# A two-block transformer kernel on one core: every tile of its scratch arena lies 32 bytes further in each partition

## The chip, the cores and the metric

The kernel runs on one NeuronCore of a Trainium2 chip. Its time is the device time of that core in microseconds (us). Two runs of the kernel before took 2086.70 and 2087.92 us, median 2087.31 us. The matmul engine (PE) has a granted clock with two levels, 2.4 GHz (shown as 1.00) and 1.2 GHz (0.50).

## The reference

Two blocks, each of two layers, over 256 tokens of width 1024; everything is float32.

```python
def reference(x, c, ctx, ...):
    x = first_block(x, c, ctx, c_ctx, w_ada, ..., w_mlp1, w_mlp2)
    return second_block(x, hyb_w_in_2, ..., ln2_g_2, ln2_b_2)

# first_block, for each of 2 layers (the 256 context tokens go along in the first, and give keys and values in the second):
#   modulation vectors   silu(c) @ w_ada[i] + b_ada[i]
#   px = modulate(rmsnorm(x)) @ w_in[i]       # conv input, q, k, v, gates
#   differential attention, conformer conv (31 taps, depthwise), gated merge, @ w_out
#   x = x + gx2 * square(relu(h @ w1)) @ w2
# second_block: layer 0 a hybrid mixer (sliding window attention + gated delta rule),
#   layer 1 a recurrent mixer (4-tap conv, gated linear scan); each followed by
#   layer_norm(alpha * x + mix) and layer_norm(alpha * x + square(relu(x @ w1)) @ w2)
```

## The kernel before

All weights stream from HBM as 273 chunks of 1 MiB through a ring of four slots, `raw_weights`. Each float32 chunk is split in two: ScalarE (ACT, L1363) rounds it to `weights_hi` in the type float32r, and VectorE (DVE, L1964) writes the rest, `weights_lo`, over the raw slot. The modulation chunks alone are used raw. Activations are split in the same way (`h_hi` and `h_lo`, and likewise o, z, ff, g, xc). A product is then three float32r matmuls into one PSUM bank: hi by hi (L652), hi by lo (L653), lo by hi (L654). The other matmuls (attention scores and values, transposes, the delta rule, the warm-up matmuls `keep_warm` at L705) are plain float32.

A matmul has a stationary operand, loaded into the array, and a moving operand, streamed through it. There are three shapes of product:

- `gemm_T` and `first_gemm`: a 128x128 piece of the weights is stationary, the activations move, 512 or 256 columns.
- `gemm_M`: a 128x128 piece of the activations is stationary, 256 columns of weights move.
- `acc_chunks` (L1017, L1018, L1021; the second block's down projections and output projections): a piece of the activations is stationary, 512 columns of weights move.

The order on each engine is written out by hand, with semaphores between the engines and hardware loops over the MLP steps. SyncE issues the chunks' transfers, each when its slot is free. No planner or cost table decides anything.

Where the tiles lie matters here. The long-lived tiles are allocated one after the other, and the allocator rounds each start up to 32 bytes. After them comes the arena, 112 KiB in each partition, in which the tiles of the stages overlay each other at whole or half KiB; its base is rounded up to 64 bytes:

```python
ARENA = 112 * 1024
arena_at = -(-nc.sbuf_base // 64) * 64

def place(name, kib, shape, dt=F32):
    size = 4 * int(np.prod(shape[1:]))
    assert kib * 1024 + size <= ARENA, (name, kib, size)
    return nc.alloc_sbuf_tensor_at(name, shape, dt, offset=int(arena_at + kib * 1024))
```

The byte addresses in a partition, worked out from these sizes:

| tile | address | past a multiple of 64 |
|---|---|---|
| raw_weights, weights_lo | 16,512 | 0 |
| weights_hi | 49,280 | 0 |
| xT (the residual tokens) | 82,048 | 0 |
| cols, rows | 98,432; 100,896 | 0; 32 |
| consts (identity, ones, tables) | 105,568 | 32 |
| small, ssq, qprod, osq_row, root | 111,136 to 112,544 | 32 |
| arena base | 114,624 | 0 |
| arena end | 229,312 | 0 |

In the arena are, among others, h_hi, h_lo, qT, kT, val, z, zc, qs, exA, exT, o_hi, o_lo, ff, ffsq, ff_hi, ff_lo, g_hi, g_lo, masks, xr, xc, outrow. Slices of these that matmuls use start at multiples of 256 bytes from the tile's start, so all of them start at a multiple of 64. VectorE's convolutions don't: z has rows of 286 elements (1,144 bytes) and its 31 taps (L2198) start 4 bytes apart; cx and xr have rows of 259 elements (1,036 bytes), four taps each (L2518, L2728), and are written 12 bytes into each row (L1710 by ACT).

Of the kernel before, what the change touches and what calls it, by code (L numbers as in the profile page):

```python
# [239 lines left out]
def build_program(nc, a):  # L240
    with ExitStack() as ctx:
# [23 lines left out]


        ARENA = 112 * 1024
        arena_at = -(-nc.sbuf_base // 64) * 64

        def place(name, kib, shape, dt=F32):  # L270
            size = 4 * int(np.prod(shape[1:]))
# [2734 lines left out]
```

## Time and profile before

| | |
|---|---|
| median of the runs | 2087.31 us |
| the profiled execution (its span, first to last instruction) | 2089.1 us |
| PE busy, share of the span | 2024.6 us, 97% |
| PE's weight loads busy | 1789.9 us, 86% |
| DVE busy | 1363.7 us, 65% |
| ACT busy | 1019.1 us, 49% |
| POOL busy | 162.3 us, 8% |
| mean granted PE clock | 0.991 |
| DMA | 294.56 MB, mean 141 GB/s |

The first line is the metric. The profiled execution is one run of the same program; no time beside its span is recorded for it, and 2089.1 is 1.8 us above the median. PE's spans overlap each other, since matmuls are pipelined, so the pace of a stream of matmuls is read from the distance between their starts, not from the duration of one.

### The profile page before, as it was taken

The page shows a single profiled execution, that of the slowest core. Times are in us where ns is not written, and L with a number is a line of the kernel's source. Part 1 is how long each engine was busy: PE and PEld are TensorE (multiplying, and loading weights), DVE is VectorE, ACT ScalarE, POOL GpSimd, SP SyncE. Part 2 cuts the span into 40 slices and gives each one's busy share as a digit, 9 for nine tenths or more (in the row PEclk, how much of TensorE's full clock was granted, in tenths as well). Part 3 has the DMA queues.
Part 4 walks back from the last instruction along what each step waited for, and adds up shares of the span by engine and source line. Part 5 has one row for each costly group of instructions (what it writes and reads, how often), then busy time and mean ns, then how long its engine had stood idle before and what let it go on. Part 6 is the DMA issues. An engine that isn't in the chain of part 4 may idle for free.

```text
span 2089.1 us, 36236 instructions
## 1 busy us (share of the span) xinstructions
PE 2024.6 (97%) x13946; PEld 1789.9 (86%) x13946; DVE 1363.7 (65%) x2114; ACT 1019.1 (49%) x2014; POOL 162.3 (8%) x174
## 2 busy tenths in 40 slices
PE   6999999999999999999999999999999999999998
PEld 5899657888788888879967999999998989888897
DVE  5699688344565564577977667776766555886455
ACT  5475575324422322358457454445824444675443
POOL 0000000000000001000000002223120111000110
PEclk9999999999999999999999999999999999999999
DMA  7322374222222222233255545554302555443553
GB/s 287 122 82 102 122 283 161 81 101 101 81 83 98 100 100 83 98 108 135 83 203 217 179 147 181 185 192 176 115 21 82 181 181 188 184 164 137 191 183 121
DMA packets 40896, 294.56 MB, mean 141 GB/s; under 512 B 4544, under 2 KB 4544, under 8 KB 5456
## 3 DMA queue, kind: packets, MB, share of 16 engines
q1 hardware_dynamic: 40464, 290.73, 38.4%
q0 software_dynamic: 320, 2.26, 0.3%
q8 instruction: 79, 1.29, 0.3%
q14 instruction: 33, 0.27, 0.0%
HBM read 291.93 MB, written 1.05 MB: 140 GB/s over the span
## 4 chain that ended last, share of the span: by engine, by line
PE 88%; DVE 5%; ACT 4%; issue 1%; DMA 1%; SPq 0%; DVEq 0%; ACTq 0%
PE psum L652 21%; PE psum L654 21%; PE psum L653 20%; PE psum L1017 3%; PE psum L1021 3%; PE psum L1018 3%; PE psum L890 2%; PE psum L1224 2%; DVE weights_lo L1964 2%; PE psum L793 2%; PE psum L912 1%; PE psum L692 1%; PE psum L693 1%; PE psum L694 1%; ACT weights_hi L1363 1%
## 5 line engine op out<-in xcount | busy, mean ns | idle before, releaser
L1964 DVE TENSOR_TENSOR weights_lo<-raw_weights,weights_hi 128x2048 fp32r<-128x2048 f32 x225 | 512.6, 2291 | 163.1 <-ACT weights_hi L1363 162.7
L1363 ACT ACTIVATE weights_hi<-raw_weights 128x2048 fp32r<-128x2048 f32 x225 | 429.0, 1910 | 152.6 <-DMA raw_weights<-in_weights 133.1
L2043 DVE SCALAR_TENSOR_TENSOR xT<-psum,mods,xT 128x256 f32<-128x256 f32 x408 | 181.0, 479 | 199.9 <-PE psum L654 196.5
L652 PE MATMUL psum<-h_hi,weights_hi 128*128 128x512 f32 (+1 forms) x832 | 279.9, 336 | 0.1
L654 PE MATMUL psum<-h_lo,weights_hi 128*128 128x512 f32 (+1 forms) x832 | 279.8, 336 | 0.0
L653 PE MATMUL psum<-h_hi,weights_lo 128*128 128x512 f32 (+1 forms) x832 | 278.1, 334 | 0.0
L2840 POOL TENSOR_TENSOR ffsq<-ff 128x256 f32<-128x256 f32 (+1 forms) x128 | 118.2, 925 | 1592.1 <-ACT ff L1450 1107.6
L652 PE MATMUL psum<-weights_hi,h_hi 128*128 128x256 f32 x704 | 197.5, 280 | 0.0
L653 PE MATMUL psum<-weights_lo,h_hi 128*128 128x256 f32 x704 | 195.5, 278 | 0.0
L654 PE MATMUL psum<-weights_hi,h_lo 128*128 128x256 f32 x704 | 195.5, 278 | 0.0
L652 PE MATMUL psum<-g_hi,weights_hi 128*128 128x256 f32 x688 | 193.7, 282 | 0.0
L654 PE MATMUL psum<-g_lo,weights_hi 128*128 128x256 f32 x688 | 192.7, 280 | 0.0
L653 PE MATMUL psum<-g_hi,weights_lo 128*128 128x256 f32 x688 | 192.5, 280 | 0.0
L652 PE MATMUL psum<-ff_hi,weights_hi 128*128 128x512 f32 (+1 forms) x512 | 172.9, 338 | 0.3 <-DVE xT L2043 0.3
L654 PE MATMUL psum<-ff_lo,weights_hi 128*128 128x512 f32 (+1 forms) x512 | 172.1, 336 | 0.0
L653 PEld LDWEIGHTS psum<-h_hi,weights_lo 128*128 128x128 f32 x832 | 156.3, 188 | 17.6
L654 PEld LDWEIGHTS psum<-h_lo,weights_hi 128*128 128x128 f32 x832 | 156.2, 188 | 17.3
L653 PE MATMUL psum<-ff_hi,weights_lo 128*128 128x512 f32 (+1 forms) x512 | 170.8, 334 | 0.0
L652 PEld LDWEIGHTS psum<-h_hi,weights_hi 128*128 128x128 f32 x832 | 156.0, 188 | 16.8 <-ACT ff L1450 0.8
L1450 ACT ACTIVATE ff<-psum 128x512 f32<-128x512 f32 (+1 forms) x64 | 31.4, 491 | 273.9 <-PE psum L654 271.6
L652 PEld LDWEIGHTS psum<-weights_hi,h_hi 128*128 128x128 f32 x704 | 132.6, 188 | 0.3 <-issue 0.2
L653 PEld LDWEIGHTS psum<-weights_lo,h_hi 128*128 128x128 f32 x704 | 132.5, 188 | 0.3 <-issue 0.2
(423 smaller groups left out, 4277.6 us busy)
## 6 DMA issues: line engine op xcount, KB each, us to landing
raw_weights<-in_weights SPq DMA_DIRECT2D x273, 1024.0 KB, 4.8
staged_x<-in_x_rows SPq DMA_DIRECT2D x1, 2048.0 KB, 10.0
masks<-in_masks POOLq DMA_DIRECT2D x1, 1152.0 KB, 6.8
ln_rows<-in_ln_rows POOLq DMA_DIRECT2D x1, 1024.0 KB, 6.8
out<-outrow SPq DMA_DIRECT2D x4, 256.0 KB, 2.1
rows<-in_rows SPq DMA_DIRECT2D x1, 584.0 KB, 9.7
consts<-in_consts SPq DMA_DIRECT2D x1, 388.0 KB, 3.8
cols<-in_cols SPq DMA_DIRECT2D x1, 306.0 KB, 2.8
```

What stands on the lines that cost most here:

```text
L652: mm(out, *pair(wh, vh), start=i == 0, stop=False)
L653: low = mm(out, *pair(wl, vh), start=False, stop=False)
L654: last = mm(out, *pair(wh, vl), start=False, stop=i == len(terms) - 1)
L793: last = mm(out[j:j + QUAD, :], cond[:, k, :], ws[c][:, k, :], start=k < 2, stop=k >= KT - 2, tile_position=(0, j))
L890: last = mm(b, qT[64 * c:64 * c + 64, h, q * P:q * P + P], kT[64 * c:64 * c + 64, h, k0 * P:k1 * P], start=True, stop=True)
L1017: mm(out, h, wh[:, k, n], start=False, stop=False)
L1018: low = mm(out, h, wl[:, k, n], start=False, stop=False)
L1021: last = mm(out, lo, wh[:, k, n], start=False, stop=final and k0 == k0s[-1] and k == 1)
L1363: f(w_hi[:, s, :], raw[:, s, :], ACT.Copy).then_inc(hi_done, 1)
L1964: tt_(w_lo[:, s, :], raw[:, s, :], w_hi[:, s, :].bitcast(F32), ALU.subtract).then_inc(lo_done, 1)
L2043: last = stt(xT[:, m, c], b[:, c], mods[:, l, which + m, v:v + 1], xT[:, m, c], ALU.mult, ALU.add)
L2840: tt_(ffsq[:, par, m, 0:T], x, x, ALU.mult).then_inc(ff_squared, 1)
```

## The change

The base of the arena is moved by 32 bytes. Sizes, overlays, instructions and their order stay as they are on every engine (7140 instructions in PE's program text, 1131 in DVE's, 871 in ACT's, 107 in POOL's, 25 in SP's, before and after); only the addresses of the arena's tiles differ. The base is 114,656 instead of 114,624, and the end 229,344. The tiles ahead of the arena (the weights' ring, xT, the constants) stay where they are.

```diff
@@ -265,7 +265,7 @@
         ARENA = 112 * 1024
-        arena_at = -(-nc.sbuf_base // 64) * 64
+        arena_at = -(-nc.sbuf_base // 64) * 64 + 32
 
         def place(name, kib, shape, dt=F32):
             size = 4 * int(np.prod(shape[1:]))
```

## Rows read from the trace of the kernel before

**Rows 1.** The page, part 1: busy us, share of the span, instructions.
```profile
PE 2024.6 (97%) x13946; PEld 1789.9 (86%) x13946; DVE 1363.7 (65%) x2114; ACT 1019.1 (49%) x2014; POOL 162.3 (8%) x174
```

**Rows 2.** The page, part 4: the chain that ended last, share by engine.
```profile
PE 88%; DVE 5%; ACT 4%; issue 1%; DMA 1%; SPq 0%; DVEq 0%; ACTq 0%
```

**Rows 3.** PE by form; out<-moving,stationary, rows*columns loaded, moving shape, count | busy us, mean ns.
```profile
L652 PE MATMUL psum<-weights_hi,h_hi 128*128 128x256 f32 x704 | 197.5, 280 | 0.0
...
L652 PE MATMUL psum<-g_hi,weights_hi 128*128 128x256 f32 x688 | 193.7, 282 | 0.0
...
L652 PE MATMUL psum<-h_hi,weights_hi 128*128 128x512 f32 x416 | 163.4, 393 | 0.0
...
L652 PE MATMUL psum<-h_hi,weights_hi 128*128 128x256 f32 x416 | 116.5, 280 | 0.1
...
L652 PE MATMUL psum<-ff_hi,weights_hi 128*128 128x512 f32 x256 | 101.4, 396 | 0.0
L1017 PE MATMUL psum<-weights_hi,ff_hi 128*128 128x512 f32 x256 | 100.9, 394 | 0.0
...
L652 PE MATMUL psum<-ff_hi,weights_hi 128*128 128x256 f32 x256 | 71.5, 279 | 0.3 <-DVE xT L2043 0.3
```

**Rows 4.** Timeline of PE, activations moving, 512 columns; start us first.
```profile
799.52 0.39 PE L653 MATMUL psum<-ff_hi,weights_lo 128*128 128x512 f32 x1
...
803.18 0.39 PE L654 MATMUL psum<-h_lo,weights_hi 128*128 128x512 f32 x1
```

**Rows 5.** Timeline of PE, activations moving, 256 columns, first layer's second half.
```profile
1169.62 0.28 PE L652 MATMUL psum<-o_hi,weights_hi 128*128 128x256 f32 x1
...
1171.98 0.28 PE L654 MATMUL psum<-o_lo,weights_hi 128*128 128x256 f32 x1
```

**Rows 6.** The same form (256 columns of activations) in the hybrid mixer.
```profile
1454.77 0.28 PE L653 MATMUL psum<-g_hi,weights_lo 128*128 128x256 f32 x1
...
1456.92 0.28 PE L654 MATMUL psum<-g_lo,weights_hi 128*128 128x256 f32 x1
```

**Rows 7.** Timeline of PE in an `acc_chunks`: weights moving, 512 columns.
```profile
1637.82 0.40 PE L1017 MATMUL psum<-weights_hi,ff_hi 128*128 128x512 f32 x1
...
1640.86 0.39 PE L1018 MATMUL psum<-weights_lo,ff_hi 128*128 128x512 f32 x1
```

**Rows 8.** Timeline of PE, plain float32, both operands in the arena.
```profile
1532.30 1.06 PE L1224 MATMUL psum<-tIT,ut 128*128 128x128 f32 x8
1533.19 1.06 PE L1224 MATMUL psum<-ut,tIT 128*128 128x128 f32 x8
```

**Rows 9.** Timeline of PE, plain float32, warm-up matmuls: both operands in consts.
```profile
1608.79 1.28 PE L705 MATMUL psum<-consts 128*128 128x128 f32 x10
```

**Rows 10.** Instructions of single lines: count, ns min/median/max, first and last start.
```profile
L2198 DVE SCALAR_TENSOR_TENSOR zc<-z,cols,zc x240: 473/608/951, 68.2 to 1049.1; 128x512 f32<-128x512 f32 x60, 128x256 f32<-128x256 f32 x60
L2728 DVE SCALAR_TENSOR_TENSOR xc<-xr,cols,xc x24: 466/472/480, 1812.0 to 1829.7; 128x256 f32<-128x256 f32 x24
L1710 ACT ACTIVATE cx<-psum x12: 361/385/390, 1449.3 to 1499.3; 128x256 f32<-128x256 f32 x12
L1511 ACT ACTIVATE kT<-psum x16: 365/384/388, 158.1 to 1021.5; 128x256 f32<-128x256 f32 x16
```

**Rows 11.** The page, part 6: DMA issues, KB each, median us to landing.
```profile
staged_x<-in_x_rows SPq DMA_DIRECT2D x1, 2048.0 KB, 10.0
...
out<-outrow SPq DMA_DIRECT2D x4, 256.0 KB, 2.1
...
consts<-in_consts SPq DMA_DIRECT2D x1, 388.0 KB, 3.8
cols<-in_cols SPq DMA_DIRECT2D x1, 306.0 KB, 2.8
```

**Rows 12.** Timeline of PE while its clock was granted at half speed.
```profile
1440.68 0.41 PE L652 MATMUL psum<-weights_hi,g_hi 128*128 128x256 f32 x1
...
1442.81 0.41 PE L653 MATMUL psum<-weights_lo,g_hi 128*128 128x256 f32 x1
```

## The prediction

> **What bounds the kernel.** I began with the busy shares [rows 1]: PE is busy for 97% of the span, and no other engine for more than 65%. The chain of waits says the same from the other side [rows 2]: 88% of the path that ended last is PE's own work, 5% DVE's, 4% ACT's, 1% transfers. So an address can cost time in two ways only: it changes the pace of matmuls, or it lengthens a DVE, ACT or DMA step of the remaining 10%. Third came the groups of PE by form [rows 3]. In those rows the reader should see which operand moves. The three lines of `product` repeat each other's counts, so activations move with 512 columns in 3 x (416 + 256 + 96) = 2,304 matmuls, where 96 is the o tiles' smaller group, and in 2,592 once the groups of `first_gemm` and z are added; with 256 columns in 3 x (688 + 416 + 256 + 96) = 4,368, and 4,896 with the smaller groups. Weights move with 256 columns in 3 x 704, 2,352 in all, and with 512 columns in 3 x 256, 959 in all. That is 10,799 float32r matmuls, and each has exactly one operand in the arena: moving in 7,488 of them, stationary in 3,311. Last, the timeline gives the pace of each form by its starts.
>
> **The paces.** Activations moving, 512 columns: 16 intervals in 803.18 - 799.52 = 3.66 us, 228.8 ns each [rows 4]. The same, 256 columns: 20 intervals in 2.36 us, 118.0 ns [rows 5]. But the same form also runs at 19 intervals in 2.15 us, 113.2 ns [rows 6]. Weights moving, 512 columns: 13 intervals in 3.04 us, 233.8 ns [rows 7]. Two things follow. A column costs (228.8 - 118.0) / 256 = 0.433 ns, which leaves 118.0 - 256 x 0.433 = 7.2 ns of fixed cost in a matmul. And an identical form has two paces 4.8 ns apart, so something beside the columns decides between them; the operands of [rows 5] and [rows 6] both lie at multiples of 64 bytes, so that something is not visible in these starts.
>
> **The change, part by part.** No instruction is added, removed or moved, so each term is a change in the duration of something that is there.
>
> *Plain float32 matmuls.* Before the change, consts already lies 32 bytes past a multiple of 64, so the trace holds the case that the change creates. With both operands in the arena, eight matmuls start 1533.19 - 1532.30 = 0.89 us before the next eight: 111 ns each [rows 8]. Warm-up matmuls with both operands in consts: 10 in 1.28 us; with the last one's 275 ns ((1.06 - 0.275) / 7 = 112 ns is the same reckoning on the arena's eight) that is (1.28 - 0.275) / 9 = 112 ns [rows 9]. A start at 32 costs neither the stationary nor the moving operand anything here. Term: 0, bounds plus or minus 1 ns on some 1,600 matmuls, 1.6 us.
>
> *Float32r matmuls.* No float32r operand lies at 32 before, so this is bounded by neighbours. The nearest row is again the plain float32 one, which reads 128 columns in 112 ns; the float32r one reads 256 columns in 113 to 118 ns, so it asks about twice as much of the memory per ns, if a plain column is read once. That is the gap through which a cost could come. I take the nearest row's value, 0. Upper end: one more unit of reading in each matmul, the line rival below; lower end: the fixed cost, below too.
>
> The Trainium skill ("SBUF — State Buffer", Specifications) says that SBUF's lines are 16 bytes, that two hits per line are needed, and that each crossing to a new line pays. A shift of 32 bytes leaves every element at the same place in its line, so by that rule the float32r term is 0 as well; no row here shows the size of a line for a float32r stream.
>
> *DVE and ACT.* The convolutions already read at every multiple of 4 bytes within 64. L2728's 24 instructions take 466 to 480 ns over their different starts, and L2198's two forms show no second level beyond a lone slow one (its minimum 473 is that of the 256-column form) [rows 10]. ACT writes cx at twelve different starts in 361 to 390 ns, and kT, whose starts are all multiples of 64, in 365 to 388. Term: 0. As a bound, 14 of 480 ns is 3%; on the 9% of the span that DVE and ACT have in the chain (188 us) that is plus or minus 5.6 us. The large splits of the chunks (L1363, L1964) lie outside the arena and don't change, whatever DVE does on arena tiles. POOL's tiles have no such row, but POOL is idle for 92% of the span [rows 1] and is no part of the chain; a few per cent on its squares stay hidden behind PE's up projection.
>
> *DMA.* The 273 chunks land outside the arena. In it land staged_x, on the path for 10.0 us, the masks and ln_rows, early and unwaited, and out leaves from it, its last part on the path for 2.1 us. consts (at 32) landed at 388 / 3.8 = 102 KB/us, cols (at 0) at 306 / 2.8 = 109 [rows 11], so 7% at most of 12.1 us: 0 to 0.9 us. I take 0.
>
> **Sum.** 2089.1 + 0 = 2089.1 us for the profiled execution, which stands 1.8 us (0.1%) above the median of the runs. I forecast 2087 us.
>
> **The rivals.** 2% of this kernel is 42 us, and is about what a measurement of it can tell from no change; the first rival stays below it.
>
> *The two paces trade places* (22%). What puts a form at 113.2 or 118.0 ns could be how its two streams of reads, the stationary and the moving, fall against each other, and that changes when one of them moves by 32 bytes and the other doesn't. For it: the two paces exist in one form [rows 5, 6]. Against it: they exist with nothing moved. If all 256-column matmuls with moving activations fell to the faster pace, 4,896 x 4.8 ns = 24 us, and the 959 weight streams went from 233.8 to 228.8, another 5 us: 2089 - 28 = 2061. If instead 2,352 weight streams went up by 4.8 ns (11 us) and 2,592 of 512 columns by 5.0 ns (13 us): 2113. Both ends are extremes.
>
> *One reading unit more in each matmul* (13%), the case on the slower side. Suppose PE fetches a float32r stream in pieces of 64 bytes, 16 columns. A start in the middle of a piece makes every stream touch one piece more, 16 x 0.433 = 6.9 ns. Place: PE, in each matmul whose activations move, 7,488 x 6.9 ns = 52 us, 2141 us; if weight loads pay too, 10,799 x 6.9 = 75 us, 2164. It decides once the fetch has no slack left, which plain float32 at half the columns per ns can't tell. Against it: all of [rows 8, 9] show not even 1 ns.
>
> *The stream runs at a fraction of its pace* (6%): every piece is fetched twice and the array starves. The far end is the pace that the row at half clock shows, 10 intervals in 2.13 us, 213 ns for 256 columns [rows 12]. For 4,896 that is +95 ns, 465 us, and for 2,592 of 512 columns twice as much, 492 us: 3046. A tenth of it gives 2185.
>
> *Faster by over 2%* (4%): the fixed 7.2 ns vanish, because the two reads no longer meet. 10,799 x 7.2 = 78 us: 2011.
>
> That the change doesn't do what it says I give nothing: the arena ends at 229,344, and all addresses in it follow from the one base.
>
> **How the numbers follow.** No change within some 8 us: 55%. With the trade of paces within 2%: 77%. Slower by over 2%: 13 + 6 = 19%. Faster by over 2%: 4%. The range goes from 2061, the low end of the trade of paces, to 2141, the line rival without the weight loads, which takes in about half of its 13%; outside are the other half, the 6% and the 4%, some 17%.
>
> **What would show it.** Right: 118 and 229 ns between starts in the same stages, 112 for plain float32 with arena operands, PE busy 2025 us, staged_x landing in 10 us. A trade of paces shows as 113 where 118 was, or the reverse, stage by stage. The line rival shows as 125 and 236 where activations move, and no change, or the same 7 ns, where weights move; plain float32 stays at 112. A fraction of the pace shows in matmul durations above 280 and 393 ns. The forecast fails if float32r reading has a unit coarser than 32 bytes that plain float32 doesn't feel.

## The result, and the profile after

The changed kernel takes 2118.86 us (median of 2 runs, 2117.6 to 2120.11) where the kernel before took 2087.31: 1.0144 times as long, with a 95% interval of 1.0119 to 1.0169. That is 31.6 us more. By the 2% bound it counts as no change; by its own interval it is slower. The profiled execution has a span of 2118.3 us against 2089.1, so 29.2 us more, and it is this difference that the traces have to explain.

Part 1 of the page gives busy us, share of the span and instructions:

```profile
PE 2058.0 (97%) x13946; PEld 1810.1 (85%) x13946; DVE 1360.7 (64%) x2114; ACT 1019.6 (48%) x2014; POOL 162.8 (8%) x174
```

Against [rows 1] the counts are the same on every engine, DVE lies 3.0 us lower, ACT and POOL 0.5 higher. PE alone is busy for 33.4 us more, and its weight loads for 20.2 us more. The chain of waits, by engine, and the landing of the first transfer:

```profile
PE 87%; DVE 7%; ACT 4%; issue 1%; DMA 1%; DVEq 0%; SPq 0%; ACTq 0%
```

```profile
staged_x<-in_x_rows SPq DMA_DIRECT2D x1, 2048.0 KB, 10.4
```

The chain is still PE's [rows 2]. staged_x lands 0.4 us later than in [rows 11], no more than a detail of 29 us. So the matmuls themselves became longer. The groups by form (out<-moving,stationary, count, busy us, mean ns of one) say where. These answer to [rows 3]:

```profile
L652 PE MATMUL psum<-weights_hi,h_hi 128*128 128x256 f32 x704 | 199.2, 283 | 0.0
...
L652 PE MATMUL psum<-g_hi,weights_hi 128*128 128x256 f32 x688 | 195.3, 284 | 0.0
...
L652 PE MATMUL psum<-h_hi,weights_hi 128*128 128x512 f32 x416 | 163.6, 393 | 0.0
L652 PE MATMUL psum<-h_hi,weights_hi 128*128 128x256 f32 x416 | 117.9, 283 | 0.1
...
L1017 PE MATMUL psum<-weights_hi,ff_hi 128*128 128x512 f32 x256 | 101.4, 396 | 0.0
```

The 256-column groups have a mean 2 or 3 ns higher, but the 512-column group of h has the 393 ns of [rows 3] (its two sister groups in L653 and L654 rose from 389 and 393 to 394 and 399). A reader who stopped at this row would think the wide matmuls untouched. They aren't: the mean duration holds a matmul's whole latency, and matmuls overlap, so a stream's cost is the distance between starts. The timeline of PE, activations moving, 512 columns (start us, us, line, operands):

```profile
812.08 0.39 PE L653 MATMUL psum<-ff_hi,weights_lo 128*128 128x512 f32 x1
...
816.28 0.39 PE L653 MATMUL psum<-ff_hi,weights_lo 128*128 128x512 f32 x1
```

18 intervals in 4.20 us are 233.3 ns each, where [rows 4] gave 228.8. The same with 256 columns:

```profile
1190.62 0.28 PE L652 MATMUL psum<-o_hi,weights_hi 128*128 128x256 f32 x1
...
1192.78 0.28 PE L652 MATMUL psum<-o_hi,weights_hi 128*128 128x256 f32 x1
```

18 intervals in 2.16 us, 120.0 ns, against 118.0 in [rows 5]. With the roles exchanged, weights moving with 256 columns, first the kernel before (a form not shown so far) and then the changed one:

```profile
149.70 0.28 PE L652 MATMUL psum<-weights_hi,h_hi 128*128 128x256 f32 x1
...
151.96 0.28 PE L654 MATMUL psum<-weights_hi,h_lo 128*128 128x256 f32 x1
```

```profile
149.95 0.28 PE L652 MATMUL psum<-weights_hi,h_hi 128*128 128x256 f32 x1
...
152.41 0.28 PE L652 MATMUL psum<-weights_hi,h_hi 128*128 128x256 f32 x1
```

20 intervals in 2.26 us are 113.0 ns, and 21 in 2.46 us are 117.1. Plain float32 stays where it was: the warm-up matmuls of [rows 9] read

```profile
1635.26 1.28 PE L705 MATMUL psum<-consts 128*128 128x128 f32 x10
```

the same 1.28 us for ten. Adding up the distances from one start to the next over all recorded float32r matmuls gives the account of the 29.2 us:

| form | count | before, us | after, us | typical ns between starts |
|---|---|---|---|---|
| activations move, 512 columns | 2,592 | 598.1 | 610.1 (+12.0) | 229.0 to 233.4 |
| activations move, 256 columns | 4,896 | 592.5 | 600.2 (+7.7) | 117.8 (some 113.3) to 120.0 |
| weights move, 256 columns | 2,352 | 274.4 | 282.5 (+8.1) | 113.3 (some 117.8) to 117.4 or 118.8 |
| weights move, 512 columns | 959 | 226.2 | 226.7 (+0.5) | 233.3 to 233.9 |
| all | 10,799 | 1691.3 | 1719.6 (+28.3) | |

28.3 of the 29.2 us lie there. The half-clock stretches are no part of it: of 38.3 us at half the granted clock before, 16.5 lay in float32r distances, and of 43.9 after, 14.4. The 0.9 us that are left are the balance of small terms outside these matmuls, of the clock among others, and no run takes them apart.

### The profile page after: what moved, and what is told of

The parts are those of the page before. It is cut to its first block, busy times and chain, and to the rows that moved or that the text cites. A ratio compares the mean times of both kernels' runs of the same rounds, so it can differ in the third digit from the quotient of the medians.

```text
span 2118.3 us, 36236 instructions
## 1 busy us (share of the span) xinstructions
PE 2058.0 (97%) x13946; PEld 1810.1 (85%) x13946; DVE 1360.7 (64%) x2114; ACT 1019.6 (48%) x2014; POOL 162.8 (8%) x174
## 3 DMA queue, kind: packets, MB, share of 16 engines
q0 software_dynamic: 320, 2.26, 0.3%
## 4 chain that ended last, share of the span: by engine, by line
PE 87%; DVE 7%; ACT 4%; issue 1%; DMA 1%; DVEq 0%; SPq 0%; ACTq 0%
PE psum L654 20%; PE psum L652 20%; PE psum L653 20%; PE psum L1017 3%; PE psum L1018 3%; PE psum L1021 3%; DVE weights_lo L1964 2%; PE psum L890 2%; PE psum L1224 2%; PE psum L793 2%; PE psum L912 1%; ACT weights_hi L1363 1%; PE psum L692 1%; PE psum L694 1%; PE psum L693 1%
## 5 line engine op out<-in xcount | busy, mean ns | idle before, releaser
L654 PE MATMUL psum<-h_lo,weights_hi 128*128 128x512 f32 (+1 forms) x832 | 283.6, 341 | 0.0
L653 PE MATMUL psum<-h_hi,weights_lo 128*128 128x512 f32 (+1 forms) x832 | 280.5, 337 | 0.0
L654 PE MATMUL psum<-weights_hi,h_lo 128*128 128x256 f32 x704 | 197.2, 280 | 0.0
L653 PE MATMUL psum<-weights_lo,h_hi 128*128 128x256 f32 x704 | 197.2, 280 | 0.0
L654 PE MATMUL psum<-g_lo,weights_hi 128*128 128x256 f32 x688 | 194.8, 283 | 0.0
L653 PE MATMUL psum<-g_hi,weights_lo 128*128 128x256 f32 x688 | 194.2, 282 | 0.0
L654 PE MATMUL psum<-ff_lo,weights_hi 128*128 128x512 f32 (+1 forms) x512 | 174.6, 341 | 0.0
L653 PEld LDWEIGHTS psum<-h_hi,weights_lo 128*128 128x128 f32 x832 | 157.3, 189 | 20.1
L653 PE MATMUL psum<-ff_hi,weights_lo 128*128 128x512 f32 (+1 forms) x512 | 172.6, 337 | 0.0
L654 PEld LDWEIGHTS psum<-h_lo,weights_hi 128*128 128x128 f32 x832 | 155.9, 187 | 18.1
L653 PEld LDWEIGHTS psum<-weights_lo,h_hi 128*128 128x128 f32 x704 | 132.6, 188 | 0.3 <-issue 0.2
```

Source lines behind the costliest of these rows:

```text
L653: low = mm(out, *pair(wl, vh), start=False, stop=False)
L654: last = mm(out, *pair(wh, vl), start=False, stop=i == len(terms) - 1)
```

## The experiments

Three theories went into the first round. **A**: a float32r operand's own start decides, in either role, so a start at 32 past a multiple of 64 is slow in itself. **B**: what decides is how the moving and the stationary start lie to each other. **C**: the pace comes from outside PE (other engines or transfers that use the same memory), and the addresses matter only through them. Below, d is the moving start minus the stationary start in bytes, modulo 256. Weights come from a ring at 16,512 (128 modulo 256), the arena lies at 114,624 (192), and its float32r tiles at multiples of 1,024 from there. So before the change d is 64 where activations move and 192 where weights move; after it d is 96 and 160.

### e1_bench

PE by itself, in streams built like the kernel's. T(m, s, n): activations move from start m, weights stationary from s, n columns; M: weights move; PL: plain float32. Each case is one line, 48 matmuls, all bases being equal modulo 256.

```
def T(mov, stat, n, reps=2):  # as gemm_T: weights stationary
    for m in range(reps):
        c = slice(m % 2 * P, m % 2 * P + P)
        terms = [(W(stat, 0, 256 * k, c), W(stat, 1, 256 * k, c), H(mov, 0, k, slice(0, n)), H(mov, 1, k, slice(0, n)))
                 for k in range(KT)]
        for x in product(terms, True):
            yield (psum[:, m % 2, 0:n], *x)
...
for o, w, v, first, end in T(64, 0, 512): last = mm(o, w, v, start=first, stop=end)
for o, w, v, first, end in T(96, 0, 512): last = mm(o, w, v, start=first, stop=end)
for o, w, v, first, end in T(0, 0, 512): last = mm(o, w, v, start=first, stop=end)
for o, w, v, first, end in T(32, 0, 512): last = mm(o, w, v, start=first, stop=end)
...
for o, w, v, first, end in T(64, 32, 512): last = mm(o, w, v, start=first, stop=end)
for o, w, v, first, end in T(96, 32, 512): last = mm(o, w, v, start=first, stop=end)
```

> PE alone: no other engine works while it runs, and the output is no result of the blocks (all of their computation is left out). Each line is one stream of float32r matmuls with the slices' addresses of the real kernel: T is gemm_T (weights stationary, activations moving), M is gemm_M; the first number is how many bytes the moving operand starts past a multiple of 128, the second the same of the stationary one. Theory A (own start): a float32r stream pays when its own start is not at a multiple of 64, in either role. Then T(96, 0, 512) is 233 ns between starts and T(64, 0, 512) 229, T(64, 32, 512) is slower than 229 as well, T(96, 32, 512) is the slowest, T(0, 0) equals T(64, 0), and T(32, 0), T(80, 0), T(68, 0) are like T(96, 0). Theory B (relative): what counts is how the moving and the stationary stream lie against each other. Then T(96, 32) equals T(64, 0), and T(64, 32) equals T(96, 0). Theory C (other engines): the loss needs traffic of the other engines; then all T of one width are alike here. Plain float32 (PL) is 112 ns at every start by all three.

Measured, timeline of PE. L86 to L89 are T(64,0), T(96,0), T(0,0) and T(32,0) with 512 columns, L92 and L93 are T(64,32) and T(96,32), L94 is T(64,0) with 256; L113 to L115 are plain float32 at (64,0), (96,0) and (96,32), two records a matmul:

```profile
43.46 11.15 PE L86 MATMUL psum<-hid,wgt 128*128 128x512 f32 x48
54.45 11.37 PE L87 MATMUL psum<-hid,wgt 128*128 128x512 f32 x48
65.66 11.07 PE L88 MATMUL psum<-hid,wgt 128*128 128x512 f32 x48
76.57 11.37 PE L89 MATMUL psum<-hid,wgt 128*128 128x512 f32 x48
...
110.21 11.35 PE L92 MATMUL psum<-hid,wgt 128*128 128x512 f32 x48
121.40 11.15 PE L93 MATMUL psum<-hid,wgt 128*128 128x512 f32 x48
132.39 5.81 PE L94 MATMUL psum<-hid,wgt 128*128 128x256 f32 x48
...
262.15 10.88 PE L113 MATMUL psum<-plain 128*128 128x128 f32 x96
272.87 10.88 PE L114 MATMUL psum<-plain 128*128 128x128 f32 x96
283.59 10.88 PE L115 MATMUL psum<-plain 128*128 128x128 f32 x96
```

A group's duration holds 47 intervals and one whole matmul, so L86 is (11.15 - 0.39) / 47 = 228.9 ns and L87 (11.37 - 0.39) / 47 = 233.6. Those are the kernel's two numbers with DVE, ACT and POOL idle and 0 to 2 GB/s of transfers, so C falls. Moving both operands by 32, L93, brings 228.9 back, where A wanted the slowest of all, so A falls; T(32,0) is as slow as T(96,0). T(0,0), with the roundest starts of all, has yet another pace, about 227. With 256 columns: 117.8 for T(64,0), 119.9 for T(96,0), and where weights move 113.3 for M(0,64) and 120.0 for M(0,96). The last is not quite the kernel's number after the change (117.4 or 118.8) at the same distance; the scan below shows 117.1 for it. Plain float32 doesn't feel it: 10.72 us from each start to the next, 111.7 ns a record.

### e2_both32

The pair of operands keeps its distance, and everything lies 32 bytes further: the change, with the ring moved along.

```diff
+        sb("pad", [P, 8])
-        ring_at = -(-nc.sbuf_base // 64) * 64
+        ring_at = -(-nc.sbuf_base // 32) * 32
...
-        arena_at = -(-nc.sbuf_base // 64) * 64
+        arena_at = -(-nc.sbuf_base // 64) * 64 + 32
```

> The change with the weights' ring, xT and the constants also 32 bytes further, so that both operands of all 10,799 float32r matmuls start at 32 past a multiple of 64. Theory A (own start): both streams pay, slower than the change's 2119 us, 2125 to 2150. Theory B (relative placement): the two lie against each other as before the change, 2087 us, with the paces 229 and 118 ns.

Measured: 2090.17 us, 1.0008 (0.9997 to 1.0019) times the kernel before, which had 2088.57 in this and the next two experiments. Page and timeline:

```profile
PE 2024.4 (97%) x13946; PEld 1789.5 (86%) x13946; DVE 1363.1 (65%) x2114; ACT 1018.8 (49%) x2014; POOL 161.9 (8%) x174
```

```profile
799.77 0.39 PE L654 MATMUL psum<-h_hi,weights_lo 128*128 128x512 f32 x1
...
803.89 0.39 PE L654 MATMUL psum<-h_hi,weights_lo 128*128 128x512 f32 x1
```

PE's 2024.6 us of [rows 1] are back within 0.2, and 18 intervals in 4.12 us are 228.9 ns again. The whole arena lies where the change put it, and costs nothing there. A had expected 2125 to 2150 us. This is the run that decides against it in the kernel itself: DVE, ACT and the transfers have the changed addresses here too, and the time is that of before.

### e3_ring32

The opposite: the arena stays, the ring moves by 32.

```diff
+        sb("pad", [P, 8])
-        ring_at = -(-nc.sbuf_base // 64) * 64
+        ring_at = -(-nc.sbuf_base // 32) * 32
```

> The arena where it was before the change, at a multiple of 64, and the weights' ring (with xT and the constants) 32 bytes further: the roles of the change turned round. Theory A (own start): weights that move pay (959 x 4.4 + 2,352 x 2.2 = 9 us) and stationary weights pay in up to 7,488 matmuls at up to 4 ns (30 us), 2096 to 2126 us. Theory B (relative): as the change, 2119 us, and with the change's paces in each form: 233 ns where 512 columns of activations move.

Measured: 2108.23 us, 1.0095 (1.0079 to 1.011).

```profile
PE 2045.5 (97%) x13946; PEld 1797.0 (85%) x13946; DVE 1361.7 (65%) x2114; ACT 1019.5 (48%) x2014; POOL 162.5 (8%) x174
```

```profile
812.00 0.39 PE L654 MATMUL psum<-ff_hi,weights_lo 128*128 128x512 f32 x1
...
816.20 0.39 PE L654 MATMUL psum<-ff_hi,weights_lo 128*128 128x512 f32 x1
```

No arena address differs from the kernel before, and yet PE is busy for 20.9 us longer. Of these, 14.5 us are float32r distances, and about 6.4 are half of the 12.9 us more that this execution spent at half the granted clock (51.2 against 38.3). The run alone doesn't exclude A, whose range for it (2096 to 2126 us) holds the measured time; e1_bench and e2_both32 do. The 512-column streams run at 4.20 / 18 = 233.3 ns as in the changed kernel. But B had expected the change's full cost, 2119 us, and missed. By the medians it came out at two thirds, and the float32r distances grow by 14.5 us and not 28.3, because 256-column streams of activations ran at 116.7 ns, faster than before, where the change has 120.0. So the distance decides, but not by whether it is an odd multiple of 32: 32 and 224 are other cases than 96 and 160. That asked for a scan, e5_scan.

### e4_ff32

One pair of tiles is moved, ff_hi and ff_lo, all else as before.

```diff
-        ffH = place("ff_hi", 48, [P, 2, 2, T2], F32R)
-        ffL = place("ff_lo", 56, [P, 2, 2, T2], F32R)
+        ffH = place("ff_hi", 48 + 1 / 32, [P, 2, 2, T2], F32R)
+        ffL = place("ff_lo", 56 + 1 / 32, [P, 2, 2, T2], F32R)
```

> The kernel before with ff_hi and ff_lo alone 32 bytes further. They move in 768 matmuls of 512 columns and 768 of 256, and are stationary in 768 of 512 columns. With the differences between the two traces (+4.4 ns, +2.2, +0.6) that is 3.4 + 1.7 + 0.5 = 5.6 us, 2093 us, by theories A and B alike, and every other tile's matmuls keep 229 and 118 ns. If the loss came from the phase of the whole program, or from another engine's tiles, 2087 us.

Measured: 2095.99 us, 1.0041 (1.0028 to 1.0054); by the medians 7.4 us, where 5.6 were expected. In the trace the streams with ff have the paces of the changed kernel (233.3 ns for 768 of 512 columns, 120.0 for 768 of 256, 234.1 where weights move), and h, g, o, z and xc those of before (229.0 and 117.8 for h). All float32r distances together grow by 5.8 us; from the paces, 768 x 4.4 + 768 x 2.2 + 767 x 0.8 ns = 5.7. The cost belongs to the pair of tiles that a matmul reads, and not to a state of the core as a whole.

### e5_scan

PE alone again, 24 matmuls each, every multiple of 32 up to 480, finer steps, and S: as T with 32 or 64 stationary columns.

```
cases=["T(64, 0, 512, 4)"]
for f,n in (('T',512),('T',256)):
    cases+=[f"{f}({m}, 0, {n}, 1)" for m in scan]
for n in (256,512):
    cases+=[f"M(0, {s}, {n}, 1)" for s in scan]
...
for n in (512,256):
    for cols in (32,64):
        cases+=[f"S({m}, 0, {n}, {cols})" for m in (0,32,64,96,68)]
```

> PE alone again (all of the blocks' computation is left out). The relative start is scanned: moving minus stationary from 0 to 480 bytes in steps of 32 for T (512 and 256 columns), stationary minus moving for M, then finer steps, then T with only 32 or 64 stationary columns (S). If the pace depends on the difference with a period of 128 bytes, T(128), T(256), T(384) equal T(0) = 226.6 ns, and T(192), T(320), T(448) equal T(64) = 228.8; with a longer period they differ. If two reads that meet are the cause, a shorter weight read meets the stream less: with 32 stationary columns every start comes within 2 ns of 216 ns for 512 columns; if the moving stream alone were the cause, S(96, 0, 512, 32) keeps 233 ns against 229 of S(64, 0, 512, 32).

Measured, timeline of PE: L94 to L97 are d = 0, 32, 64, 96, L98 is 128, L102 to L106 are 256, 288, 320, 352 and 384, all with 512 columns:

```profile
43.61 5.63 PE L94 MATMUL psum<-hid,wgt 128*128 128x512 f32 x24
49.08 5.77 PE L95 MATMUL psum<-hid,wgt 128*128 128x512 f32 x24
54.68 5.67 PE L96 MATMUL psum<-hid,wgt 128*128 128x512 f32 x24
60.18 5.77 PE L97 MATMUL psum<-hid,wgt 128*128 128x512 f32 x24
65.80 5.76 PE L98 MATMUL psum<-hid,wgt 128*128 128x512 f32 x24
...
88.21 5.63 PE L102 MATMUL psum<-hid,wgt 128*128 128x512 f32 x24
93.67 5.77 PE L103 MATMUL psum<-hid,wgt 128*128 128x512 f32 x24
99.28 5.67 PE L104 MATMUL psum<-hid,wgt 128*128 128x512 f32 x24
104.78 5.77 PE L105 MATMUL psum<-hid,wgt 128*128 128x512 f32 x24
110.39 5.76 PE L106 MATMUL psum<-hid,wgt 128*128 128x512 f32 x24
```

5.63, 5.77, 5.67, 5.77, 5.76 us, and the same five from 256 on, while 128 (5.76) is not 0 (5.63): the pattern repeats after 256 bytes and not after 128. So do the 256-column streams (d = 192 and 448: the same 113.3 ns). In ns between starts, over the second half of each stream, since the first matmuls are still settling (over all 23 intervals d = 0 has 227.8):

| d, bytes | 0 | 32 | 64 | 96 | 128 | 160 | 192 | 224 |
|---|---|---|---|---|---|---|---|---|
| 512 columns | 226.7 | 233.3 | 228.9 | 233.3 | 233.3 | 234.3 | 233.3 | 233.3 |
| 256 columns | 120.0 | 117.7 | 117.8 | 120.1 | 118.7 | 117.3 | 113.3 or 117.8 | 118.3 |

With the roles exchanged the 512-column row is the same function of d: M(0,192), d = 64, gives 228.9, M(0,64), d = 192, 233.3, M(0,96), d = 160, 234.2. With 256 columns too M(0,160), d = 96, has 120.0 and M(0,96) 117.1, but there a distance doesn't always give one pace: d = 160 ran at 120.0 in the first experiment, and d = 192 at 113.3 in T and 117.8 in M. Off the multiples of 32 it goes further: 236.7 ns at d = 4, 240.0 at 68, which in the first experiment ran at 236.7. The table turns e3_ring32's miss round. For d = 32 it has 233.3 and 117.7, for 224 it has 118.3 and 233.3, and that kernel showed 233.3, 116.7, 118.3 and 233.3. The streams with fewer stationary columns answered nothing. With 32 of them the 512-column streams ran at 231.5, 233.5, 231.7 and 233.3 ns (d = 0, 32, 64, 96), neither all alike nor as with 128, and nowhere near the 216 ns that were expected. With 512 columns the differences become smaller when less is loaded; with 256 columns they don't (32 stationary columns: 113.3 ns at d = 0 and 64, 117 at 32 and 96). That part is inconclusive.

### e6_d0

By the table the roundest choice, d = 0 in all streams, is best for 512 columns and worst for 256. The arena goes to 114,560; for that the four columns of lam move into cols.

```diff
-        cols = sb("cols", [P, COLS_N])
+        cols = sb("cols", [P, COLS_N + 4])
-        lam = sb("lam", [P, 4])
+        lam = cols[:, COLS_N:COLS_N + 4]
-            sp.dma_start(cols[:, :], a["cols"]).then_inc(loaded, 16)
+            sp.dma_start(cols[:, 0:COLS_N], a["cols"]).then_inc(loaded, 16)
```

> The arena 64 bytes lower, at 114,560, a multiple of 128 (lam is kept in four spare columns of cols to make room), so that activations and weights start at the same place in 256 bytes. If the pace is a function of moving minus stationary start modulo 256 and nothing else, as the scan with PE alone gave it (E5), the difference is 0 in every float32r matmul: 226.7 ns where 512 columns of activations move (-2.2 x 2,592 = -5.7 us), 120.0 where 256 columns of activations move (+2.2 x 4,896 = +10.8), 120.0 where 256 of weights move (+5.3 x 2,352 = +12.4), 226.7 where 512 of weights move (-6.6 x 959 = -6.3): +11 us, ratio 1.0054, slower although the base is at a rounder address. If a rounder start is what helps (theory A with a unit of 128), 2087 or faster.

Measured: 2098.83 us, 1.0059 (1.0038 to 1.008), where the table had given 1.0054; the kernel before had 2089.23 in this and the next two.

```profile
800.03 0.39 PE L652 MATMUL psum<-h_hi,weights_hi 128*128 128x512 f32 x1
...
803.88 0.39 PE L654 MATMUL psum<-h_lo,weights_hi 128*128 128x512 f32 x1
```

17 intervals in 3.85 us, 226.5 ns: the wide streams gain 2, as in L88 of the first experiment, and all 256-column ones go to 119.9, which costs more. The profiled execution is shorter than the median says (span 2091.1) for a reason of its own: it spent 24.9 us at half the granted clock where the profile of before spent 38.3. Its float32r distances stand only 7.4 us above before's. Of the time at half clock 6.5 and 16.5 us lay in them, so (16.5 - 6.5) / 2 = 5.0 us more would be there at equal clock, 12.4 in all where the table had 11.2. This is the first run that turns the paces of the bench into a forecast of the kernel, and it held; of the three that follow, two missed.

### e7_ff192

Now the table is used to gain. ff is read at 512 columns in both roles, and d = 0 is the best there for both; moving ff_hi and ff_lo by 192 bytes gives it to them alone.

```diff
-        ffH = place("ff_hi", 48, [P, 2, 2, T2], F32R)
-        ffL = place("ff_lo", 56, [P, 2, 2, T2], F32R)
+        ffH = place("ff_hi", 48 + 3 / 16, [P, 2, 2, T2], F32R)
+        ffL = place("ff_lo", 56 + 3 / 16, [P, 2, 2, T2], F32R)
```

> The kernel before with ff_hi and ff_lo alone 192 bytes further: the difference to the weights becomes 0 there. By the scan 226.7 instead of 228.9 ns in 768 matmuls (-1.7 us), 120.0 instead of 117.8 in 768 (+1.7) and 226.7 instead of 233.3 in the 768 in which ff is stationary and 512 columns of weights move (-5.1): -5 us, ratio 0.9976. By theory A no change.

Measured: 2087.66 us, 0.9994 (0.9984 to 1.0003). A miss: 0.9976 was expected. The paces of ff came nearly as expected (227.8, 120.0 and 228.1 ns), which is worth 768 x 1.1 + 767 x 5.2 - 768 x 2.2 ns = 3.1 us. But the float32r distances fell by only 1.2 us. Part of the rest is a pace that no address of this experiment touches. The first h stream of the kernel, 185 matmuls of 512 columns from 42 to 85 us, runs here at

```profile
59.67 0.40 PE L652 MATMUL psum<-h_hi,weights_hi 128*128 128x512 f32 x1
...
66.90 0.40 PE L653 MATMUL psum<-h_hi,weights_lo 128*128 128x512 f32 x1
```

31 intervals in 7.23 us, 233.2 ns, where it had 228.9 or 229.0 in the traces of before, e2_both32, e4_ff32, e8_best and e10_g48, at the same d = 64. ff is first read at 568 us, so it can't be the cause; what is, no run shows. That costs 0.8 us. The h streams that come between those of ff lose 0.3 ns a matmul (229.2). The weights-moving streams of g ran at 116.4 instead of 113.7, but they had 115.6 in e2_both32 too, with every d as before. So a stream's pace is not fixed by its d alone, and single effects of about 1 us can't be read from one profile of each kernel.

### e8_best

e7_ff192, and in addition the tiles g_hi and g_lo are moved by 128 bytes, to bring their 2,208 matmuls of 256 columns from d = 64 to 192, the case with a pace of 113.3.

```diff
-        gH = place("g_hi", 0, [P, KT, SEQ], F32R)
-        gL = place("g_lo", 8, [P, KT, SEQ], F32R)
-        masks = place("masks", 16, [P, MASKS_N])
+        gH = place("g_hi", 1 / 8, [P, KT, SEQ], F32R)
+        gL = place("g_lo", 8 + 1 / 8, [P, KT, SEQ], F32R)
+        masks = place("masks", 16 + 1 / 8, [P, MASKS_N])
-        xr = place("xr", 16, [P, KT, SEQ + B_CONV - 1])
+        xr = place("xr", 16 + 1 / 8, [P, KT, SEQ + B_CONV - 1])
```

> As E7, and g_hi and g_lo 128 bytes further (masks and xr, which follow them in the arena, too), so that in the second block's 2,064 matmuls of 256 moving columns of g the difference is 192. In the scan that difference ran at 113.3 ns as T and at 113.3 or 117.8 as M. If all of it runs at 113.3: -9.3 us beside E7's -5, ratio 0.993; if it runs at 117.8: E7's 0.9976.

Measured: 2086.17 us, 0.9989 (0.998 to 0.9999), where 0.993 or 0.9976 was expected: a miss. The g streams stayed near their slow pace, 116.5 ns in the mean, down from 117.3, so most of the hoped gain didn't come. d = 192 has two paces, and these streams mostly take the slower one.

### e9_pairs

PE alone, on two questions. Which weight load counts, a matmul's own or that of the next, which runs beside it? And what chooses between 113.3 and 117.8? PAIR(x, a, y, b) alternates a matmul moving from x with weights at a and one from y with weights at b.

```
def PAIR(x, a, y, b, n, reps=24):  # two streams and two weight pieces in turn
    for i in range(reps):
        yield (psum[:, 0, 0:n], W(a, 0, 0, slice(0, P)), H(x, 0, 0, slice(0, n)), i == 0, False)
        yield (psum[:, 0, 0:n], W(b, 1, 0, slice(0, P)), H(y, 0, 1, slice(0, n)), False, i == reps - 1)
...
for m in (192,16,240,208,176,48,112,144,12,20,160):
    cases+=["PL(0, 0, 128, 5)",f"T({m}, 0, 256, 1)","T(64, 0, 512, 1)",f"T({m}, 0, 256, 1)"]
```

> PE alone (all of the blocks' computation is left out). PAIR(x, a, y, b): two matmuls in turn, moving at x with weights at a, then moving at y with weights at b. If a matmul's stream meets the weight load of the next matmul, which runs beside it, the differences x - b and y - a count: PAIR(0, 0, 96, 96, 512) runs at the pace of the differences 96 and 160 (233.3 to 234.3 ns) and PAIR(0, 96, 96, 0, 512) at that of 0 (226.7). If its own weights count, it is the other way round. PAIR(0, 0, 0, 0) is 226.7 by both. The rest of the lines look for what chooses between the two paces of one difference at 256 columns: T(192, 0, 256) once behind five plain matmuls and once behind 512-column ones. If the start decides, the two differ (113.3 and 117.8), and differences with one pace alone (0, 96) would not.

Measured, timeline of PE; L99 is (0,0,0,0), L100 (0,0,96,96), L101 (0,96,96,0), L102 (96,0,96,0), L103 (0,0,160,160), with 512 columns:

```profile
44.09 11.05 PE L99 MATMUL psum<-hid,wgt 128*128 128x512 f32 x48
54.98 11.39 PE L100 MATMUL psum<-hid,wgt 128*128 128x512 f32 x48
66.21 11.20 PE L101 MATMUL psum<-hid,wgt 128*128 128x512 f32 x48
77.24 11.37 PE L102 MATMUL psum<-hid,wgt 128*128 128x512 f32 x48
88.45 11.38 PE L103 MATMUL psum<-hid,wgt 128*128 128x512 f32 x48
```

In L100 each matmul lies at d = 0 to its own weights, and at 160 or 96 to the next one's. It runs at (11.39 - 0.39) / 47 = 234.0 ns, the slow pace: a matmul's own weights don't set it. In L101 it lies at d = 0 to the next one's, and at 230.0 it is neither 226.7, which that rule wants, nor slow. So it is mostly the other matmul's weights, which fits a load that runs beside the stream, but not that alone. In a pair that alternates, the next matmul's weights are also the last one's, so these cases can't tell the two apart. With 256 columns the four mixed pairs ran at 117.8, 116.7, 118.3 and 116.7 ns, which fits neither rule well.

The second question. L112 and L114 are the same stream, T(192,0) with 256 columns, behind plain float32 matmuls and behind a 512-column stream; their last 18 and 16 matmuls:

```profile
146.61 2.20 PE L112 MATMUL psum<-hid,wgt 128*128 128x256 f32 x18
```

```profile
154.97 2.05 PE L114 MATMUL psum<-hid,wgt 128*128 128x256 f32 x16
```

(2.20 - 0.28) / 17 = 112.9 ns and (2.05 - 0.28) / 15 = 118.0. One instruction stream with one set of addresses has two lasting paces, and what ran before it picks one. d = 112 gave 113 to 114 behind either predecessor where activations move; where weights move, the same d, M(0,144), has 120.0.

The wide streams have it too. T(64,0) with 512 columns stands twelve times in this run. Eleven times it settles at 228.8 or 228.9 ns; behind T(20,0) with 256 columns it stays at (5.77 - 0.40) / 23 = 233.5:

```profile
259.09 5.77 PE L149 MATMUL psum<-hid,wgt 128*128 128x512 f32 x24
```

And the kernel before shows it at d = 64 with 256 columns: g's stream at 1621 us, behind plain float32 matmuls, settles at 113.3 ns, and the 28 that each follow a 512-column stream of ff run at 117.8. The predecessor's kind alone doesn't say which, though: h's streams at 1145 and 1151 us follow plain float32 as well and settle at 117.8.

### e10_g48

e7_ff192, with g at d = 112, the distance that had no slow pace where activations move: g_hi and g_lo begin 48 bytes further. Tiles are placed at multiples of 32 only, so they are placed 32 further and used from their fifth column on.

```diff
-        gH = place("g_hi", 0, [P, KT, SEQ], F32R)
-        gL = place("g_lo", 8, [P, KT, SEQ], F32R)
-        masks = place("masks", 16, [P, MASKS_N])
+        past = lambda x: x[:, 4:4 + KT * SEQ].rearrange("p (k t) -> p k t", k=KT)
+        gH = past(place("g_hi", 1 / 32, [P, 4 + KT * SEQ], F32R))
+        gL = past(place("g_lo", 8 + 1 / 32, [P, 4 + KT * SEQ], F32R))
+        masks = place("masks", 16 + 1 / 16, [P, MASKS_N])
-        xr = place("xr", 16, [P, KT, SEQ + B_CONV - 1])
+        xr = place("xr", 16 + 1 / 16, [P, KT, SEQ + B_CONV - 1])
```

> As E7 (ff 192 bytes further), and g_hi and g_lo 48 bytes further instead of E8's 128 (a tile 32 bytes further, used from its fifth element; masks and xr 64 bytes further), which makes the difference 112 where g moves. With PE alone that difference came to 113 to 114 ns behind either predecessor, where 192 kept 113.3 or 117.8 by its start. 2,208 matmuls from 117.3 to 113.8: -7.7 us; 240 in which g is stationary from 113.7 to 120.0 (the difference 144): +1.5. With E7's own -1.2 us of the traces: -7 us, ratio 0.9965. If the paces are not carried over from PE alone, E7's ratio 0.9994.

Measured: 2080.78 us against 2089.23, 0.9954 (0.994 to 0.9967); 0.9965 was expected.

```profile
1689.96 0.28 PE L653 MATMUL psum<-g_hi,weights_hi 128*128 128x256 f32 x1
...
1692.23 0.28 PE L655 MATMUL psum<-g_lo,weights_hi 128*128 128x256 f32 x1
```

20 intervals in 2.27 us, 113.5 ns; the mean over all g streams is 114.2, where before has 117.3. The float32r distances fall by 11.1 us, the span by 10.1. This version is faster than both kernels, by addresses alone.

## Why the prediction was wrong

The forecast was 2087 us. The measured 2118.86 lies in the range (2061 to 2141), and by the 2% bound it is in the case with 77%. But the likeliest case, no change within 8 us, had 55% and didn't happen.

*What bounds it, and the count.* Held. PE was the bound, and an address could cost only through the pace of matmuls or through the rest of the chain; all but 0.9 us of the difference was of the first kind. The 10,799 float32r matmuls counted are the ones whose distances grew by 28.3 us.

*Plain float32, DVE, ACT, DMA: 0.* Held. Plain matmuls have 111.7 ns in all four combinations of e1_bench. DVE's busy time is 3.0 us lower and ACT's 0.5 higher. staged_x landed 0.4 us later (forecast 0, bound 0.9). e2_both32 has all these at their changed addresses, and its time is within 0.2% of before.

*Float32r matmuls: the step that failed.* The term was set to 0 by the plain float32 row: "A start at 32 costs neither the stationary nor the moving operand anything here." True of that row, and e1_bench bears it out. It was the wrong neighbour, in two ways. It was of the other kind of matmul, which shows no effect of the start at any d that was tried (0, 32, 64 and 96); the prediction named the gap itself ("it asks about twice as much of the memory per ns") and then took the row's value all the same. And it was read as a statement on one operand's start, while the kernel's cost depends on the distance of two. At the row's value the term was 0, measured it was +28.3 us.

A rule had stood beside that term: the Trainium skill ("SBUF — State Buffer", Specifications) has lines of 16 bytes, within which a shift of 32 changes nothing, so by it too the term is 0. The measurement differs, and decides: 4.4 ns in 229 from a shift of 32 bytes, and d = 0, 64 and 128, each a whole number of such lines, have three paces, 226.7, 228.9 and 233.3 ns. A rule and a row agreed here, and both were about something else.

*The trade of paces, 22%.* This rival had the mechanism: "how its two streams of reads, the stationary and the moving, fall against each other". e1_bench and e2_both32 show it, with PE alone and in the kernel. What failed in it are the bounds. They allowed each form only the two paces already seen, so at most 2113, and left the 4,896 matmuls of 256 columns no way up, since 118.0 was the slower one known. There was a third pace, 120.0 ns, and it gave 7.7 us. The two terms that the upper bound did have were 13 us for the wide streams and 11 us for the 256-column weight streams; 12.0 and 8.1 were measured. 2113 and 7.7 would have been 2121. The row that spoke against it, two paces with nothing moved [rows 5, 6], was a true observation of a second effect, the two lasting paces at one d (e9_pairs), and no evidence against the first.

*One reading unit more, 13%.* It expected 125 and 236 ns where activations move, measured were 120.0 and 233.3. It fell in e2_both32 above all: every start in the arena is in the middle of its supposed piece there, for nothing. That its range end, 2141, made the range wide enough was luck of the size, not a reason.

*The fraction of the pace (6%), the fixed cost gone (4%).* No form's mean duration is near 280 + 95 ns, and no form's pace fell.

*The size of what can be told.* The prediction took 42 us to be about what a measurement can tell from no change. The intervals of these runs reach 0.1 to 0.25% to either side, 2 to 5 us, so the 31.6 us stand well clear of them.

The Trainium skill ("TensorE: Matmul & The Clock Gate", Step-by-step: what each phase is for) says that PE reaches SBUF by two independent ports, one for the moving data and one for weights. By that the pace can't hang on a difference of the two addresses, and the trade of paces could not have happened. The trace does not agree for float32r: T(96,32) is 228.9 ns and T(96,0) 233.6, with PE alone, only the weights' start differing. For plain float32 it agrees (111.7 each).

Shown: the change's cost comes from the relative start of the two operands (e1, e2 and e3, where the starts are shifted by 32 bytes, and e5), the period of 256 bytes (e5), and the cost per tile pair (e4). A forecast from the table held in e6 and e10, and missed in e7 and e8, by some 3 us or more, where a stream took the slower of its two paces or an untouched one changed. Only partly shown: that it is the load beside the stream which meets it (e9 excludes the own weights as the only cause, and fits the other matmul's weights in the first pair but not in the second). Open: why 256 bytes, why the order of the paces isn't the same for 256 and 512 columns, and what picks one of two paces.

## What to carry to other kernels

In a kernel that PE bounds with float32r matmuls, the start of the moving tile minus that of the stationary tile, modulo 256 bytes, is a parameter worth 3% of a matmul of 512 columns and 6% of one of 256 (1.4% of this kernel); read it from the addresses, and measure the pace per form, role and distance with PE alone, behind more than one predecessor, before placing tiles; then measure the kernel (two of four such forecasts missed here), since rounding to 64 or 128 is no answer (e6_d0 is slower). When an edit shifts addresses, shift both operands by the same amount or neither. When the price of an unseen case is taken from the nearest row, ask first whether that row shows an effect of this kind at all: a row that can't respond is no evidence of 0.

## What the runs showed of the hardware that was not expected

- The pace of a float32r stream depends on the difference of two addresses: 226.7 to 234.3 ns for 512 columns at multiples of 32, up to 240.0 at d = 68; 113.3 to 120.1 ns for 256 columns. Plain float32 has 111.7 ns for 128 columns, 429.2 for 512, at every start that was tried.
- One stream of 256 columns at d = 192 has two lasting paces, 113.3 and 117.8 ns, chosen by what ran before it, and d = 160 was seen at 117.1 and at 120.0. At d = 64 it is 113.3 and 117.8 for 256 columns (before) and 228.9 and 233.3 for 512 (e9_pairs, e7_ff192). So a stage whose addresses stay can run at another pace, in e7_ff192 from 42 us on, before anything that differs from the kernel before has run.
- Time at half the granted clock differs between executions of nearly the same program: 38.3 us in the profile of before, 24.9 in that of e6_d0. At half speed that is 6.7 us, as much as several of the effects here, so the paces and not the spans have to carry such a comparison.
